# A hybrid decoder layer on one Trainium2 core: the dense pass paced in slots by the kind of its ticks

## The reference, cut to what matters

```python
def peer_ffn(h, w_q, sub_keys, u, v):
    ...                                  # scores of the two halves of the keys, top 16 of each, top 16 of the sums
    expert = i1 * PEER_N_KEYS + i2
    gates = jax.nn.softmax(best, axis=-1)
    ...
    def per_block(inp):
        xb, eb, gb = inp
        act = jnp.einsum('bthkd,btd->bthk', u[eb], xb).astype(jnp.float32)
        w = (gb * jax.nn.gelu(act, approximate=False)).astype(v.dtype)
        return jnp.einsum('bthk,bthkd->btd', w, v[eb])
    ...

def reference(...):
    ...
    ff = peer_ffn(h, peer_wq[l], peer_keys[l], peer_u[l], peer_v[l])
    h = layer_norm(DEEPNORM_ALPHA * h + ff, ln3_g[l], ln3_b[l])
```

## Time and profile before

| | |
|---|---|
| median of three runs | 3981.11 us (3973.81 to 3985.49) |
| the profiled execution | 3994.52 us; its span is 3992.7 us, 1.8 us lie around it |
| PE, DVE, ACT, POOL busy | 79%, 53%, 23%, 45% of the span |
| DMA | 1,076 MB, mean 269 GB/s over the span |
| mean granted clock of PE | 0.863 of full speed |
| gathers (issued by POOL) | 805.4 MB; other loads and stores 268.4 MB |
| chain that ended last | DMA 20%, PE 16%, DVE 11%, POOL 10%, issue 7% of the span |

### The profile page before, as it was taken

The page is one execution under the profiler, slowest core; times in us unless marked ns, Lnnn a source line. Parts: engine busy times, 40 slices in busy tenths (PEclk is TensorE's granted clock), DMA queues, the critical chain, the costliest instruction groups (busy, mean ns, idle before and its releaser), DMA issues.

```text
span 3992.7 us, 39638 instructions
## 1 busy us (share of the span) xinstructions
PE 3157.8 (79%) x13938; PEld 1983.3 (50%) x13938; DVE 2110.2 (53%) x4574; ACT 912.3 (23%) x2677; POOL 1781.8 (45%) x1592
## 2 busy tenths in 40 slices
PE   8999968989879466565565643899999899999994
PEld 5778856656555332232232220665555576555551
DVE  2250037666400677777777777763334385343334
ACT  1320122323202122332333321221111122111111
POOL 1243200000000266666666666456666645566665
PEclk8999988999989777787787776689999979999996
DMA  2322242111032399999999999589999978999998
GB/s 76 136 92 90 89 155 93 46 65 57 32 142 113 130 357 361 347 353 367 339 359 349 359 389 357 205 331 409 409 409 409 409 261 333 409 409 409 409 409 304
DMA packets 313630, 1076.00 MB, mean 269 GB/s; under 512 B 33248, under 2 KB 56672, under 8 KB 311792
## 3 DMA queue, kind: packets, MB, share of 16 engines
q0 software_dynamic: 221184, 805.40, 53.1%
q1 hardware_dynamic: 92272, 268.37, 17.7%
HBM read 1037.47 MB, written 36.18 MB: 269 GB/s over the span
## 4 chain that ended last, share of the span: by engine, by line
DMA 20%; PE 16%; DVE 11%; POOL 10%; issue 7%; another core or an unknown queue 2%; ACT 1%; POOLq 0%; DVEq 0%; ACTq 0%
DMA u_ring<-in_u_dram,idx 12%; DMA v_ring<-in_v_dram,idx_v 9%; POOL v_ring L1432 5%; POOL u_ring L1420 5%; PE acc L1464 4%; DVE u_ring L1823 4%; PE small L1563 3%; PE small L1575 3%; PE wide L1587 3%; PE small L1518 1%; PE wide L1489 1%; DVE work L2077 1%; DVE work L2034 0%; PE wide L1503 0%
## 5 line engine op out<-in xcount | busy, mean ns | idle before, releaser
L1420 POOL DMA_INDIRECT u_ring<-in_u_dram,idx x768 | 772.8, 1006 | 1226.4 <-DVE idx L2039 800.0
L1432 POOL DMA_INDIRECT v_ring<-in_v_dram,idx_v x768 | 859.1, 1119 | 561.7 <-PE acc L1464 259.1
L1464 PE MATMUL acc<-v_ring,spread_w 128*32 128x512 f32 x3072 | 504.9, 780 | 496.1 <-DMA v_ring<-in_v_dram,idx_v 377.2
L1823 DVE CUSTOM_DVE_ANT_0 u_ring<-u_ring,h 128x1024 f32<-128x1024 f32 x406 | 495.7, 1224 | 673.2 <-DMA u_ring<-in_u_dram,idx 649.9
L1823 DVE CUSTOM_DVE_ANT_0 u_ring<-u_ring,wide 128x1024 f32<-128x1024 f32 x362 | 439.2, 1217 | 174.0 <-DMA u_ring<-in_u_dram,idx 123.5
L1464 PEld LDWEIGHTS acc<-v_ring,spread_w 128*32 128x32 f32 x3072 | 104.7, 129 | 788.8 <-issue 635.2
L1575 PE MATMUL small<-pwq 128*128 128x256 f32 x2048 | 471.0, 383 | 1.9 <-issue 0.9
L1587 PE MATMUL wide<-pwq,memory_tables 128*128 128x512 f32 x1024 | 465.4, 598 | 0.0
L1575 PEld LDWEIGHTS small<-pwq 128*128 128x128 f32 x2048 | 388.4, 191 | 131.3 <-issue 83.9
L1587 PEld LDWEIGHTS wide<-pwq,memory_tables 128*128 128x128 f32 x1024 | 192.2, 191 | 224.5 <-issue 220.1
L1654 ACT ACTIVATE spread_w<-comb,w_v 128x32 f32<-128x32 f32 x768 | 198.3, 311 | 324.3 <-remote 177.4
(11 more groups left out here) (320 smaller groups left out, 4264.1 us busy)
## 6 DMA issues: line engine op xcount, KB each, us to landing
pwq<-in_uT_dram SPq DMA_DIRECT2D x128, 512.0 KB
pwq<-in_v_dram SPq DMA_DIRECT2D x128, 512.0 KB
w_nat<-in_w_nat_dram SPq DMA_DIRECT2D x6, 2048.0 KB, 8.5
nat_dram<-stage SPq DMA_DIRECT2D x48, 256.0 KB, 2.2
u_ring<-in_u_dram,idx POOLq DMA_INDIRECT x768
v_ring<-in_v_dram,idx_v POOLq DMA_INDIRECT x768
scanT_dram<-stage SPq DMA_DIRECT2D x22, 512.0 KB, 2.9
w_tr<-in_w_tr_dram SPq DMA_DIRECT2D x18, 512.0 KB, 4.0
```

The source lines that it names most:

```text
L1420: pool.indirect_dma_start(out=u_ring[:, g % U_RING, :], out_offset=None, in_=peer_u, in_offset=bass.IndirectOffsetOnAxis(ap=idx[:, t % KEP ...
L1432: pool.indirect_dma_start(out=v_ring[:, g % V_RING, :], out_offset=None, in_=peer_v, in_offset=bass.IndirectOffsetOnAxis(ap=idx_v[:, t % K ...
L1464: last = pe.matmul(acc[c * QUAD:(c + 1) * QUAD, half * 512:(half + 1) * 512], spread_w[:, slot, :], v_ring[:, slot, half * 512:(half + 1) ...
L1823: dve.tensor_tensor_reduce(out=row, in0=row, in1=against, scale=1.0, scalar=0.0, op0=ALU.mult, op1=ALU.add, accum_out=act_u[:, (n // TOPK) ...
```

## The change

`tick_slot` no longer lays all ticks evenly. It counts units: a tick that spreads gates has SPREAD_PACE = 2 units, a tick of expert blocks has one, so that a half has 2 x 16 + 128 = 160 units, and the 320 units are laid evenly on the same 368 slots, 1.15 slots to a unit. A tick that spreads gates gets 2.3 slots in place of 1.28, and one of expert blocks 1.15 in place of 1.28. `ticks_at` becomes the inverse of `tick_slot`. The ticks, their order, their operations, waits and bytes are the same, and so are the first and the last slot of the pass. The first group of gate ticks lies in slots 384 to 420 in place of 384 to 404, the second in 568 to 604 in place of 568 to 588; the second half still begins at slot 568.

```diff
 HALF_TICKS = GROUP_TICKS + 2 * HALF_KEYS
+SPREAD_PACE = 2
+HALF_UNITS = SPREAD_PACE * GROUP_TICKS + 2 * HALF_KEYS
...
+        def tick_slot(tick):
+
+            b, r = tick // HALF_TICKS, tick % HALF_TICKS
+            units = b * HALF_UNITS + SPREAD_PACE * min(r, GROUP_TICKS) + max(r - GROUP_TICKS, 0)
+            return DENSE_AT + units * (DENSE_END - DENSE_AT) // (2 * HALF_UNITS)
+
         def ticks_at(slot):
 
-            span = DENSE_END - DENSE_AT
-            first, last = (-(-(slot + d - DENSE_AT) * 2 * HALF_TICKS // span) for d in (0, 1))
-            return range(first, last) if DENSE_AT <= slot < DENSE_END else range(0)
-
-        def tick_slot(tick):
-
-            return DENSE_AT + tick * (DENSE_END - DENSE_AT) // (2 * HALF_TICKS)
+            return [tick for tick in range(2 * HALF_TICKS) if tick_slot(tick) == slot]
```

## The result

The changed kernel took 3943.43 us in the median (3933.57 to 3945.65, four runs), the kernel before 3982.52 us over its four runs beside them (3973.81 to 3985.49). The ratio is 0.9901, with a 95% interval of 0.9878 to 0.9924: 39 us less, where 50 were forecast (3931 us, range 3903 to 3970). The profiled execution took 3943.93 us, its span is 3942.1 us, with the same 39,638 instructions.

A forecast was written before the change was run, and what follows sets the result against it. Bytes were taken to bound the expert stretches, DVE and PE together the gate stretches, with DMA partly idle. Terms -80 + 24 + 6 = -50 us on 3981.1 gave 3931 us, range 3903 to 3970.

The forecast's parts named there:

- What bounds the stretches: Dense pass: expert stretches last as long as their bytes; in gate stretches DVE and PE hold each other, DMA partly idle.
- Part 1: Expert stretches: each loses 16.4 slots of gathered work and shortens with its bytes; -80 us for both, between -84 and -72.
- the hiccup: Expert stretches: an allowance of 2 us per stretch for hiccups of the PE and POOL loop, bounds 0 and 6.
- The sign that I named: First expert stretch: PE's waits for `v` rows would be fewer than 40 us, from 44.2.
- PE's margin: Expert stretches: PE stays behind the bytes, its margin per four slots halving from 1.5 to 0.7 us.
- Rival B: Expert stretches: PE becomes the bound, gain only 20 us per stretch; sum -10, 3971 us; chance 0.10.
- Part 2: Gate stretches: 16.4 more slots each, ticks of 7.8 us; +11.9 us each, +24 for both, between +8 and +40.
- Part 3: First gate stretch: the norm of tile 3 falls into it, where DVE is the limit; +6 us, bounds +4 and +10.
- The wait that I only bounded: First gate stretch: `norm3_a` waits for the `combine` of slot 403, behind `choose` calls; covered only by bounds +4 and +10.
- Rival A: Gate stretches: thinner `choose` calls leave TensorE at 1.2 GHz, 9.0 us per tick, +31 each; 3969 us; chance 0.12.
- Rival C: Expert stretches: PE's waits for `v` rows are a ring round trip and all 44.2 us stay; 3996 us; chance 0.06.
- Rival D: Dense pass: spacing in slots changes no spacing in time, as engines drift by several slots; 3981 us; chance 0.02.

The follow-up runs named there:

- the first pair of profiles: Profiled executions of the kernel before and the changed kernel, before the follow-up runs: 3994.5 us and 3943.93 us.
- the runs: Follow-up runs, each with the kernel before beside it; the changed kernel repeated there took 3817.14 us against 3860.31.
- pace 2: SPREAD_PACE = 2, the changed kernel; repeated without edit it took 3817.14 us against 3860.31 for the kernel before, ratio 0.988.
- pace 3: Changed kernel with SPREAD_PACE = 3 in place of 2: 3823.50 us against 3868.23 for the kernel before, ratio 0.9878.
- the run of pace 1: Changed kernel with SPREAD_PACE = 1, the old spacing: 3866.28 us against 3868.23 for the kernel before, ratio 1.000.

## Why the prediction was right, and where its sizes were off

- **What bounds the stretches: right.** Expert stretches follow bytes: half the bytes of `v` shortened them to 514 us, half the products of `dense_v` left them at 543. Gate stretches follow DVE: a cheaper `hots` took 13 to 15 us away, half of `choose` 2 to 4.
- **Part 1, expert stretches, forecast -80, measured -73 in the first pair of profiles and -76 in the runs.** The first stretch came to 545.0 where the bytes gave 541.2 and the hiccup 2. The second is the larger miss, -35 for -40: I scaled its 578.2 us as bytes too, but at the old spacing it moved 2.7 MB less than the first, and at pace 2 both end at 542 to 545 us with 221 to 222 MB. So it lost 13.5 MB, 33 us at 407 GB/s, and not the 17.2 MB of 16.4 slots. The sign that I named came true: 18.3 us of PE's waits for `v` rows, under 40.
- **PE's margin: right in kind.** Priced at 14.0 of 14.7 us per four slots, or 516 us; PE's program measured 514.9. Rival B is out at pace 2 and comes in from pace 3.
- **Part 2, gate stretches, forecast +12 each, measured +14.3 in the first pair and +11.8 in the runs, in the second stretch, which has no norm.** Pairs in the second stretch stood 7.95 us apart on average (7.73 in the run) for the 7.8 forecast. I left half of the wait for `choose`; less stayed (2.0 and 4.4 us of 12), and waits for `u` rows, 7.2 us in the second stretch, took its place. I had written that the DMA does not limit there; on average it doesn't, but DVE stood four times for rows there, which I had put at nothing.
- **Part 3, the norm, forecast +6, measured +7** (21.3 less 14.3) and +6.0 in the runs (17.8 less 11.8). The wait that I only bounded is real, 5.7 us, and it went mostly over into another when removed. That +6, the norm's work alone, came so near is in part luck: the work (6.1 us) and the wait together are more, and the shorter waits of the first stretch for `choose` and for rows (3.8 us against 11.6) make up for it.
- **Rival A (clock): wrong here.** The granted clock rose, from 0.63 to 0.70, with the denser `combine` calls, and did not matter (half of `choose` at 0.60 ran no slower). The Trainium skill's rule on waits between bursts (TensorE: Matmul & The Clock Gate, HAM oscillation) fits the traces only in part. In the changed kernel the clock went from 1.00 to 0.50 by 2568 us, behind a wait of PE of 2.72 us. In the kernel before it also went from 1.00 to 0.50 by 2568 us, behind a wait of 0.73 us, and it stayed at 0.50 from 2516.4 to 2537 us, in which PE had no wait at all. The sum of the rival, 3969, is not what came.
- **Rival C (round trip of the `v` ring): out.** PE's waits fell from 44.2 to 18.3 us with the slots, and were none with half the bytes of `v`; they were slack.
- **Rival D (no effect): out.** POOL issued 72 gathers in the first gate stretch in place of 39, and 298 in place of 327 in the expert stretch behind it.
- **The sum.** In the first pair every term came out dearer than forecast, by 7, 5 and 1 us, and these make up the 12.5 us between -50 and the -37.5 of the profiled pass. No step failed; the terms that were mis-sized most are the second expert stretch (5 us) and the gate stretches of the first pair (2.3 us each). In the runs the pass gave -46.0 and the medians -43.

## What to carry to other kernels

Where a fixed amount of gathered work is interleaved with stages of different limits, price one slot of it in each stage and move slots until both prices are equal: here 2.1 to 2.5 us (bytes) against 0.7 to 1.1 us (the dot and the norm on DVE, less the waits that they fill) at the old spacing. The gain ends not where the average load of the target stage is full but earlier, at a DMA share of 0.85 and 0.89 here, when the stage's price per slot jumps to that of the source stage. A single pair of profiles can differ by 10 us in stages that nothing touched, so take the difference inside the stretches that changed.

## What the runs showed of the hardware

The stage ahead of the dense pass, whose DMA is nearly all gathers, ran at different speeds in the first pair and in the runs; the expert stretches didn't. A stretch of that stage in the kernel before, then in the run of pace 1 (same columns as above):

```profile
1600.00:2400.00 800.00, 470.88 (x2392) 226.68 (x2389) 617.33 (x1794) 256.23 (x816) 533.13 (x525) 0.75 0.96 358
...
1600.00:2300.00 700.00, 446.29 (x2256) 210.75 (x2254) 599.84 (x1804) 244.34 (x789) 518.54 (x514) 0.76 1.02 402
```

358 against 402 GB/s, DMA share 0.96 against 1.02, while both had 406 to 407 GB/s in the expert stretches. The changed kernel in the first pair gave 357 GB/s, and runs on the two chips of the experiments 401 to 403. That is most of the 3982 against 3868 us of the same kernel. Whether it is the chip wasn't looked for. And TensorE was busy for 92% of the first gate stretch, with products of 64 columns, at a mean clock of 0.63, and for 92% of the first expert stretch, with products of 256 and 512 columns, at 0.98. In the gate stretch 96 records of 64 columns ran for 20.75 us without a gap, at a granted clock of 0.50 all through; later in the stretch it rose from 0.55 to 1.00 as a `combine` ended.
